# Routed experts on TensorE: 64-token halves with strips for tokens 64 to 96, and the small experts at other places

## The reference, cut to what matters

```python
logits = (xf @ router_w).astype(jnp.float32)          # 256 tokens, 8 experts
top_logits, top_idx = lax.top_k(logits, TOP_K)        # TOP_K = 2
gates = jax.nn.softmax(top_logits, axis=-1)
...
def swiglu(h, w_gate, w_up, w_down):
    return (jax.nn.silu(h @ w_gate) * (h @ w_up)) @ w_down
...
ys = lax.map(expert_block, (xs, blk_e)).reshape(P, D) * slot_gate[:, None]
return jnp.zeros((N, D), h.dtype).at[slot_tok].add(ys)
```

## Time and profile before

| what | value |
|---|---|
| device time, three runs | 1378.35 us median, 1376.2 to 1378.42 |
| device time of the profiled execution | 1377.18 us |
| its span in the trace | 1375.3 us |
| instructions in the span | 39781, of which 18759 matmuls and 18759 weight loads |
| busy: PE, PEld, DVE, ACT | 95%, 67%, 25%, 24% |
| HBM over the span | 303 GB/s mean; 415 MB read |
| mean granted clock of TensorE | 0.988 |

### The profile page before, as it was taken

How to read it: one execution, slowest core, us unless ns; L and a number is a source line. 1 busy time by engine, 2 the same in 40 slices (tenths; PEclk the granted TensorE clock), 3 DMA queues, 4 the chain that set the end, 5 groups by cost and what they waited for, 6 DMA issues and landing times.

```text
span 1375.3 us, 39781 instructions
## 1 busy us (share of the span) xinstructions
PE 1303.9 (95%) x18759; PEld 927.0 (67%) x18759; DVE 342.7 (25%) x664; ACT 326.9 (24%) x699; POOL 0.2 (0%) x4
## 2 busy tenths in 40 slices
PE   6999999999999899999999999899989989999997
PEld 6786999997877656665666665565666565566565
DVE  5666555555585500010010000010001001001000
ACT  5665544444576300010000010010000001000000
POOL 0000000000000000000000000000000000000000
PEclk9999999999999999999999999999999999999999
DMA  9903454463511469999999999999999999999991
GB/s 363 390 24 123 157 190 143 141 239 130 184 62 61 185 258 373 373 341 399 403 408 408 401 408 407 395 408 409 378 409 407 386 405 387 407 402 408 408 365 41
DMA packets 127063, 418.88 MB, mean 305 GB/s; under 512 B 3376, under 2 KB 8112, under 8 KB 126768
## 3 DMA queue, kind: packets, MB, share of 16 engines
q1 hardware_dynamic: 126896, 416.29, 78.6%
HBM read 415.23 MB, written 1.05 MB: 303 GB/s over the span
## 4 chain that ended last, share of the span: by engine, by line
PE 87%; DVE 3%; ACT 3%; issue 3%; DMA 2%; SPq 1%; DVEq 0%; ACTq 0%
PE ps L816 37%; PE ps L803 18%; PE ps L502 7%; PE ps L504 7%; PE ps L503 7%; DMA ring<-moe_g 2%; PE ps L892 2%; PE ps L835 1%; PE ps L484 1%; SPq L461 1%; DVE scratch L1359 1%; PE ps L630 1%; ACT scratch L1012 1%; PE ps L635 1%; PE ps L638 1%
## 5 line engine op out<-in xcount | busy, mean ns | idle before, releaser
L816 PE MATMUL ps<-ring,xgT 128*32 128x256 f32 (+1 forms) x8096 | 404.0, 358 | 18.0 <-issue 17.6
L816 PEld LDWEIGHTS ps<-ring,xgT 128*32 128x32 f32 x8096 | 256.0, 111 | 158.3 <-issue 27.3
L803 PE MATMUL ps<-ring,hidT 128*32 128x256 f32 x3840 | 221.4, 382 | 11.3 <-issue 10.2
L803 PEld LDWEIGHTS ps<-ring,hidT 128*32 128x32 f32 x3840 | 126.1, 110 | 94.5 <-issue 21.5
L1634 DVE TENSOR_TENSOR hT<-ps,hT 128x768 f32<-128x768 f32 (+3 forms) x32 | 24.7, 771 | 634.5 <-PE ps L816 634.5
L816 PE MATMUL ps<-more_ring,xgT 128*32 128x256 f32 (+1 forms) x2656 | 124.8, 344 | 6.5 <-issue 3.2
L1467 DVE TENSOR_TENSOR d_lo<-ring,d_hi 128x1024 fp32r<-128x1024 f32 x82 | 100.3, 1225 | 95.0 <-ACT d_hi L1120 94.7
L1161 ACT ACTIVATE hidT<-ps 128x768 f32<-128x768 f32 (+3 forms) x32 | 21.2, 662 | 432.2 <-PE ps L835 432.2
L1120 ACT ACTIVATE d_hi<-ring 128x1024 fp32r<-128x1024 f32 x82 | 87.3, 1064 | 111.9 <-PE ps L504 111.9
L816 PEld LDWEIGHTS ps<-more_ring,xgT 128*32 128x32 f32 x2656 | 81.0, 110 | 46.7 <-issue 9.8
L502 PE MATMUL ps<-hT_hi,d_hi 128*128 128x256 f32 x352 | 99.7, 283 | 1.0 <-DVE hT_lo L1247 1.0
(11 more groups left out here) (243 smaller groups left out, 1204.3 us busy)
## 6 DMA issues: line engine op xcount, KB each, us to landing
ring<-moe_d SPq DMA_DIRECT2D x46, 2048.0 KB, 21.1
ring<-moe_u SPq DMA_DIRECT2D x45, 2048.0 KB, 24.2
ring<-moe_g SPq DMA_DIRECT2D x41, 2048.0 KB, 23.1
more_ring<-moe_g SPq DMA_DIRECT2D x15, 2048.0 KB, 24.1
more_ring<-moe_u SPq DMA_DIRECT2D x11, 2048.0 KB, 24.2
more_ring<-moe_d SPq DMA_DIRECT2D x10, 2048.0 KB, 19.5
ring<-w_in SPq DMA_DIRECT2D x6, 2048.0 KB, 10.9
ring<-dense_g SPq DMA_DIRECT2D x5, 2048.0 KB, 7.8
```

The lines of the kernel that those rows point to most:

```text
L803: ins = pe.matmul(ps[q * STRIP:(q + 1) * STRIP, 4 + t // 2, t % 2 * T:(t % 2 + 1) * T], hidT[:, c // 2 % 2, x0:x0 + STRIP], w[:, j * D + q ...
L816: ins = pe.matmul(ps[q * STRIP:(q + 1) * STRIP, b0 + b, c0:c0 + wide], xgT[:, k, t * STRIP:(t + 1) * STRIP], w[:, i * cols + q * wide:i * ...
```

## The change

With HALF = 64 and HALVES = 2, the first 64 tokens of every expert are one stationary operand of 64 columns. Two matmuls lie beside each other, each with half of the weight columns: 512 streamed columns for chunks 0 to 2 and for down, 256 for chunk 3. Tokens 64 to 95, which only big experts have, keep the strips: one stationary operand of 32 columns, four matmuls beside each other, as before. In each unit of a big expert all matmuls of the halves come first and all of the strip after them. The results lie in other places of PSUM, with as many elements: the halves fill one bank, the strip half of the next one.

The selection matrix of the gates follows: two groups of 128 columns in place of three (a small expert has one, but place 7 keeps the second, set to zero by a memset, because the last scatter always works as for a big expert). So gates_T transposes 4 or 2 blocks in place of 6 or 4. The scatter takes 64 rows at a time for the halves (8 matmuls) and 32 rows for the strip (8 more) in place of 24, and for a small expert 8 in place of 16. The small experts stand at places 1, 4 and 7 in place of 1, 3 and 6. The units, their DMAs and slots are the same.

```diff
+HALF, HALVES = 64, 2
 STRIP, STRIPS = 32, 4
 N_FULL = 5
-SMALL_AT = (1, 3, 6)
+SMALL_AT = (1, 4, 7)
...
                         for j in range(CH // P):
-
                             if c < NCH - 1:
-                                quarter, part, parts = c % 2 * 2 + j // 2, j % 2, 2
+                                x0 = j * P + c % 2 * HALF
                             else:
-                                quarter, part, parts = j, 0, 1
-                            for t in range(nt):
-                                x0 = (t * parts + part) * P + quarter * STRIP
-                                for q in range(STRIPS):
-                                    ins = pe.matmul(ps[q * STRIP:(q + 1) * STRIP, 4 + t // 2, t % 2 * T:(t % 2 + 1) * T],
-                                                    hidT[:, c // 2 % 2, x0:x0 + STRIP],
-                                                    w[:, j * D + q * T:j * D + (q + 1) * T],
...
+                                x0 = j % 2 * P + j // 2 * HALF
+                            for q in range(HALVES):
+                                ins = pe.matmul(ps[q * HALF:(q + 1) * HALF, 4, :], hidT[:, c // 2 % 2, x0:x0 + HALF],
+                                                w[:, j * D + q * CH:j * D + (q + 1) * CH], start=c == 0 and j == 0,
+                                                stop=c == NCH - 1 and j == CH // P - 1, skip_group_check=True)
+                        for j in range(CH // P if nt == BIG else 0):
...
+                            for q in range(STRIPS):
+                                ins = pe.matmul(ps[q * STRIP:(q + 1) * STRIP, 5, 0:T], hidT[:, c // 2 % 2, x0:x0 + STRIP],
+                                                w[:, j * D + q * T:j * D + (q + 1) * T], start=c == 0 and j == 0,
+                                                stop=c == NCH - 1 and j == CH // P - 1, skip_group_check=True)
...
-                        cols = GU_COLS[c]
-                        wide, b0 = cols // STRIPS, 0 if kind == "g" else 2
-                        for i in range(UNIT // cols):
-                            k = h * (UNIT // cols) + i
-                            for t in range(nt):
-                                b, c0 = divmod(t * wide, CH)
-                                for q in range(STRIPS):
...
+                        cols, ks = GU_COLS[c], UNIT // GU_COLS[c]
+                        wide, b0 = cols // HALVES, 0 if kind == "g" else 2
+                        for i in range(ks):
+                            k = h * ks + i
+                            for q in range(HALVES):
+                                ins = pe.matmul(ps[q * HALF:(q + 1) * HALF, b0, 0:wide], xgT[:, k, 0:HALF],
+                                                w[:, i * cols + q * wide:i * cols + (q + 1) * wide],
+                                                start=k == 0, stop=k == KD - 1, skip_group_check=True)
+                        b, c0 = divmod(wide, CH)
+                        for i in range(ks if nt == BIG else 0):
+                            k = h * ks + i
+                            for q in range(STRIPS):
+                                ins = pe.matmul(ps[q * STRIP:(q + 1) * STRIP, b0 + b, c0:c0 + wide // 2],
+                                                xgT[:, k, HALF:HALF + STRIP],
+                                                w[:, i * cols + q * wide // 2:i * cols + (q + 1) * wide // 2],
+                                                start=k == 0 and c0 == 0, stop=k == KD - 1, skip_group_check=True)
...
+                for a in range(TT):
+                    for n in range(2):
+                        for q in range(HALVES):
+                            rows_q = slice(q * HALF, (q + 1) * HALF)
+                            ins = pe.matmul(ps[:, SCATTER_BANKS[q * 2 + n], a * T:(a + 1) * T],
+                                            pick_gT[rows_q, a * P:(a + 1) * P], y[rows_q, n * T:(n + 1) * T],
+                                            start=a == 0, stop=nt == LITTLE, skip_group_check=True)
+                for a in range(TT if nt == BIG else 0):
+                    for q, bank in enumerate(SCATTER_BANKS):
...
```

More of the change, by code:

```diff
@@ L288, in trunk_program @@
             pick = sb_stage("pick", [P, TT, GROUP], F32R)
-            pick_g = sb_stage("pick_g", [P, TT, BIG, STRIPS, STRIP])
-            pick_gT = sb_stage("pick_gT", [P, BIG * TT * P])
+            pick_g = sb_stage("pick_g", [P, TT, 2 * P])
+            pick_gT = sb_stage("pick_gT", [P, 2 * TT * P])
             xn_hi = sb_stage("xn_hi", [P, TT, D], F32R)
@@ L372, in strips, with groups @@
             return LITTLE if g == 0 and s in SMALL_AT else BIG
+        def groups(g, s):
+            return strips(g, s) - 1 if g or s < NE - 1 else 2
         def strips_before(g, s):
@@ L796, in unit @@
                             if c < NCH - 1:
-                                quarter, part, parts = c % 2 * 2 + j // 2, j % 2, 2
+                                x0 = j * P + c % 2 * HALF
                             else:
-                                quarter, part, parts = j, 0, 1
-                            for t in range(nt):
-                                x0 = (t * parts + part) * P + quarter * STRIP
-                                for q in range(STRIPS):
-                                    ins = pe.matmul(ps[q * STRIP:(q + 1) * STRIP, 4 + t // 2, t % 2 * T:(t % 2 + 1) * T],
-                                                    hidT[:, c // 2 % 2, x0:x0 + STRIP],
-                                                    w[:, j * D + q * T:j * D + (q + 1) * T],
-                                                    start=c == 0 and j == 0 and t % 2 == 0,
-                                                    stop=c == NCH - 1 and j == CH // P - 1, skip_group_check=True)
-                    else:
-                        cols = GU_COLS[c]
-                        wide, b0 = cols // STRIPS, 0 if kind == "g" else 2
-                        for i in range(UNIT // cols):
-                            k = h * (UNIT // cols) + i
-                            for t in range(nt):
-                                b, c0 = divmod(t * wide, CH)
-                                for q in range(STRIPS):
[L816 to L819, removed]
@@ new lines, in unit @@
+                                x0 = j % 2 * P + j // 2 * HALF
[4 more added lines that the diff above has]
+                        for j in range(CH // P if nt == BIG else 0):
+                            if c < NCH - 1:
+                                x0 = (4 + j % 2) * P + (c % 2 * 2 + j // 2) * STRIP
+                            else:
+                                x0 = 2 * P + j * STRIP
+                            for q in range(STRIPS):
+                                ins = pe.matmul(ps[q * STRIP:(q + 1) * STRIP, 5, 0:T], hidT[:, c // 2 % 2, x0:x0 + STRIP],
+                                                w[:, j * D + q * T:j * D + (q + 1) * T], start=c == 0 and j == 0,
+                                                stop=c == NCH - 1 and j == CH // P - 1, skip_group_check=True)
+                    else:
+                        cols, ks = GU_COLS[c], UNIT // GU_COLS[c]
[14 more added lines that the diff above has]
+                                                start=k == 0 and c0 == 0, stop=k == KD - 1, skip_group_check=True)
@@ L839, in gates_T @@
                     pe.wait_ge(act_done, at((g, s, "hidT", 1), it))
-                    for t in range(strips(g, s)):
+                    for t in range(groups(g, s)):
                         for a in range(TT):
                             j = t * TT + a
-                            ins = pe.transpose(ps[:, 6 + j // 4, j % 4 * P:(j % 4 + 1) * P],
-                                               pick_g[:, a, t, :, :].rearrange("p q i -> p (q i)"), ident)
+                            ins = pe.transpose(ps[:, 6, j * P:(j + 1) * P], pick_g[:, a, t * P:(t + 1) * P], ident)
                     ins.then_inc(pe_done, pe_p.step((g, s, "pick_g_T")))
@@ L886, in scatter @@
             def scatter(nt):
[L888 to L895, removed]
+                for a in range(TT):
[7 more added lines that the diff above has]
+                    for q, bank in enumerate(SCATTER_BANKS):
+                        rows_q = slice(q * STRIP, (q + 1) * STRIP)
+                        ins = pe.matmul(ps[:, bank, a * T:(a + 1) * T], pick_gT[rows_q, (TT + a) * P:(TT + a + 1) * P],
+                                        y[rows_q, CH:CH + T], start=False, stop=True, skip_group_check=True)
                 return ins
@@ L1163, in expert @@
                         if c == 1:
-                            w = nt * TT * P
+                            w = groups(g, s) * TT * P
                             act.wait_ge(pe_done, at((g, s, "pick_g_T"), it))
@@ L1608, in picks @@
                                                 ALU.is_equal).then_inc(dve_done, dve_p.step((g, key, "pick")))
```

(13 more changed lines are left out.)

## The result

The changed kernel takes 1353.47 us in the median of four runs (1352.9 to 1354.13), the kernel before 1378.38 us in the same comparison. The profiled execution took 1353.37 us with a span of 1351.6 us, 23.7 less than before. Executions of the kernel before lie between 1374.45 and 1382.47 us over all comparisons, and one of 6755 us is left out of them, so a single time of it is good to a few us.

What follows compares the result with a forecast made beforehand. TensorE sets the end, loads close behind: last unit 1363.4 - 38.0 (stops) + 28.1 (form changes) - 1.7 (fewer gates_T transposes) = 1351.8, plus 11.9 of tail = 1363.7. That is 11.6 under the span, so 1367 us, range 1355 to 1380.

Steps and rivals of the forecast that it cites:

- the tail: Behind TensorE's last unit, to the end of the span: 11.9 us, forecast to stay.
- the loads' own bound: Earliest end if the expert loads set it, at 5.28 us a unit: 1357 to 1361 us.
- The stops in chunk 3 go: TensorE's "issue" stops in and behind chunk 3 vanish except for 2.4 us: -38.0 us, bounds 0 to -40.4.
- rival 4: Chunk 3's stops don't come from the number of instructions; half or more stay: 1386 us or more, chance 0.07.
- The array changes form more often: In units and scatters, 181 new changes of TensorE's form at 0.155 us: +28.1 us, bounds 0 to 32.6.
- rival 2: No emptying of the array between 64 and 32 columns; loads set the end: 1355 to 1359 us, chance 0.22.
- The streamed work stays: In the experts' units, two halves share the array as perfectly as four strips, loads hidden: no change in time.
- rival 5: A half's load isn't hidden with two beside each other: +300 us at most, 1397 at a tenth, chance 0.04.
- rival 3: Leaving the halves in big experts' units costs 0.11 to 0.22 us more at 105 changes: 1378 to 1390, chance 0.14.
- TensorE's own sum is the same: Over all experts, the new order of places leaves TensorE's total work unchanged.
- The places: Small experts at places 1, 4 and 7 save some 8 us of load waits with faster experts, about nothing alone.

Runs made afterwards that it cites:

- run 3: Changed kernel, but a big expert's unit following one that ended with its strip, no other form between, begins with the strip: 1347.81 us, ratio 0.9781.
- run 5: Changed kernel with nearly all of the strips' matmuls left out (tokens 64 to 95 get one step of each sum): 1336.63 us, ratio 0.9698.
- run 8: Kernel before, each load from the 19th unit of the experts on bringing only a quarter of its unit: 1335.81 us in one run.
- run 7: Changed kernel with the halves of chunk 3 cut into four pieces of 64 streamed columns, the same streaming: 1383.14 us in one run.
- run 4: Changed kernel with halves and strip of big experts' down units taking turns at each of four steps, 210 more form changes: 1383.16 us in one run.
- run 2: Changed kernel with the small experts back at places 1, 3 and 6: 1365.29 us, ratio 0.9915.
- run 6: Changed kernel with nearly all strip matmuls left out and each matmul of a half cut into two of half the columns: 1337.67 us, ratio 0.9711.
- run 1: Kernel before with only the small experts moved to places 1, 4 and 7: 1379.93 us, ratio 1.0015.

## Why the prediction was wrong

**The mechanism held, the sizes didn't add up.** The direction, what TensorE's units would look like (5.3 to 5.6, measured 5.45; small 3.4 to 3.5, measured 3.43), the experts' times (123.8 and 81.9, measured 122.6 to 123.9 and 81.7), the missing waits for DMAs and the worth of the places were as forecast. The time was not, and two steps failed. In the sum, four terms were wrong on the same side: the stops (by 3 us), the changes of form (2.2), the streamed work (3.4, put at nothing) and the tail (2.6). And the loads' own bound of 1357 to 1361 us, which closed the range from below, was wrong: with the loads setting the end, the runs took 1348 and 1337 us (runs 3 and 5).

**"The stops in chunk 3 go": -38.0 us.** All of them went. Light loads alone (run 8) end the last unit of the kernel before at 1322.6 in place of 1363.4 us, 40.8 us earlier, though its work is the same. This is good to about 1 us: run 8 begins its experts 3.7 us later, but at the full clock, where the kernel before has a granted clock of 0.50 until about 489 us. Beside the idle time, the stops had a price that the prediction didn't name: behind two of them, of 2.87 us at place 2 and 2.31 at place 6, the granted clock fell to its lower level for some 3 us (0.61 from 793.6 to 797.0 us, 0.57 from 1229.5 to 1233.5). The first cost 1.4 us, 98 records in 4.22 us where 128 take 3.70; the second lies in down matmuls, which the sum from the earlier trace rows left out. In the changed kernel the clock is 1.00 at all these places. The 2.4 us that I kept for chunk 3 were 0.04 us a unit (5.49 for 5.45), 0.6 in all. The cause that I gave holds: as many instructions with halves bring the stops back (run 7), and free DMA engines take them away (run 8). That they come from matmuls of 128 columns on strips (rival 4) has fallen.

**"The array changes form more often": +28.1 us.** 181 changes at 0.143 us (run 4) are 25.9. The choice between the transposes' 0.155 and the scatter's 0.18 was right in tending down, and the lower bound of nothing (rival 2) has fallen. The Trainium skill says in "TensorEngine Tiling (Array Packing)", section "Key Properties", that a change of mode drains TensorE. This case's runs agree for two widths of columns too, as far as the price of a change goes: 0.13 us (run 3) and 0.143 us (run 4).

**"The streamed work stays."** Nearly: a small unit takes 3.43 in place of 3.45 us, and a big one without its two changes 5.45 - 0.29 = 5.16 in place of 5.18. 168 units by 0.02 us are 3.4 us, which I had at nothing. With this, a half's load is hidden (rival 5 has fallen), and leaving the halves costs no more than 0.143 us (rival 3 has fallen). So 1363.4 - 41 - 1.7 + 25.9 - 3.4 = 1343.2, against 1342.3 measured. One term is still missing: "TensorE's own sum is the same" in the other order overlooked that a big expert's scatter (2.80 us) now stands before the last unit in place of a small one's (1.94), which adds 0.9. Terms read from one execution each don't close better than this, to some 2 us.

**The tail.** I let it stay at 11.9 us; it is 9.3. Before, 1.15 us of "issue" lay ahead of the last scatter, and its 48 records took 4.65 us, for the most part at the lower clock; now it is 0.04 us of "issue" and 32 records in 3.12 us at the full clock. In run 2, with the changed kernel's code, the tail is 12.3 us again, at the full clock but with 2.6 us of "issue". So the tail depends on whether the next instructions are there and on the granted clock; what decides either at that place was not tried.

**"The loads' own bound: 1357 to 1361" failed as a step.** It set the range's lower end (1355 with rival 2), and the result lies below. Run 3 ends by the loads at 1348 us, and the changed kernel by TensorE at 1353. Three parts of it were too high: the pace of 5.28 us (5.21 measured; 138 units make 9 us of it), which I had read over a stretch with dips in the DMA rate where the slots were full (SyncE waits 10.7 us for TensorE near 1100 us, at place 5, and the rate falls to about 200 GB/s) and with the end of the loads in it (2.27 MB in the last 9 us); the tail (2.6 us); and an issue at 607 us plus a whole 10.2 us for a load, though the queue always has others under way. I had seen that and taken off only 4 us. That the pace is 5.21 and not 5.25 as before is for the most part accounted for: of the 2.09 MB between the two rows (run 5), 0.83 MB are instruction packets (1.57 MB before, 0.74 after), and the rest goes with such dips, since without them both kernels run at 5.2. Twice the instructions in the halves (run 6) made no difference in time that could be told.

**The places** are worth 11.8 us with the halves (run 2 against the changed kernel; 8 predicted; in the profiled executions 8.9, of which 3.0 are in the tail, where the forecast had none) and nothing without them (run 1: 1.0015), as forecast. Halves and places together bring 24.9 us, the halves alone 12 (run 2, against 1377.6 in the same comparison): the experts must be fast enough for the loads to be missed, before it matters where a small one stands.

## What to carry to other kernels

Where an engine's stretches of "issue" follow a fixed number of its instructions (here 128 matmuls and their loads) and DMA engines are full, look at the supply of instructions: here fewer, wider instructions with the same streaming took the stops away, and so did lighter DMA traffic. Stops also cost clock: the engine may come back at its lower level, as it did behind two of them and in the last scatter. Each change between forms of TensorE's array costs 0.14 us here, so put blocks of the same form next to each other; letting every other unit begin with the form that the last one ended with brought another 5.7 us. When two resources end within a few us of each other, measure the bound of the second (leave the first one's work out) before a range is closed with it; its mean rate over a stretch with full buffers is not its pace.

## What the runs showed of the hardware that was not expected

Weight loads of 64 columns with two matmuls beside each other are hidden as well as those of 32 columns with four: 3.43 us for 16 records of 512 columns, 3.45 for 64 of 256. The supply of instructions under full loads was one packet of 128 matmuls and their weight loads in 6.2 to 6.6 us (3.70 + 2.87 at place 2, 3.70 + 2.51 at places 4 and 5), only 5 to 11% faster than the normal units used them (128 x 54 ns = 6.9 us): the kernel before ran close to this limit everywhere and showed it only in and right behind chunk 3.
